# Halving the rounding of streamed weights, moving the root-table load, and single last results

## Chip, cores, metric

The kernel runs on one core of a Trainium2 chip. The metric is the device time of one execution in microseconds (us), the median of the runs shown. The profile is one further execution, taken by the hardware profiler. TensorE is PE in it (PEld its weight loads), VectorE is DVE, ScalarE is ACT, GpSimd is POOL, SyncE is SP.

## What is computed

Two networks in a row on 512 tokens of width 1024, all in float32. The first block is a feed-forward, then a mixer (RWKV-7 recurrence beside dilated attention), then a second feed-forward:

```python
x = x + 0.5 * swiglu(rms_norm(x, ffn1_norm), ffn1_w_in, ffn1_w_out)
h = rms_norm(x, mix_norm)
p_rwkv, p_q, p_k, p_v, p_gate = _split_last(h @ w_in, ...)
merged = g_a * (y_a @ w_proj_rwkv) + g_b * (y_b @ w_proj_attn)
x = x + merged @ w_out
x = x + 0.5 * swiglu(rms_norm(x, ffn2_norm), ffn2_w_in, ffn2_w_out)
```

The second block has two layers that also carry 256 context tokens (attention with low-rank and grouped keys, a convolution over 31 tokens, gates), and a last norm:

```python
for l in range(DEPTH_2):
    x, ctx = hybrid_layer(x, ctx, ...)
return rms_norm_2(x, final_norm_w)
```

`rms_norm` takes for each token the square root of the mean of squares. That root is what the word root table is about.

## The kernel before

Activations lie channels down, tokens across: `X` is 128 partitions x 8 tiles x 512 tokens, `XC` the context.

**Weights are streamed.** All weights of all stages are one stream of 336 blocks, each of 8 tiles (`UNITS`) of 128x128, 512 KB. Every block goes the same way through four engines, with two buffers for each step (slot = block number mod 2):

- SP fetches it into `RAW` (L2631) when POOL has finished the block two before (semaphore `split`).
- ScalarE copies it to `WHI`, rounded to the matmul's format (`round_block`, L312), when the fetch has landed and TensorE has used the block two before (`blocks_used`).
- POOL subtracts: `WLO` = `RAW` - `WHI`, the rest that rounding left (L2643 for the first two, L2647 in a loop), and raises `split`.
- TensorE waits for `split` in `block_ready` and forms the product in `product`: for each tile three matmuls, L324 (high weights, high activations), L325 (high, low) and L326 (low, high).

ScalarE's rounding isn't a program of its own. Each stage's scalar function calls `round_block` at fixed points of ScalarE's order, between the stage's own operations. So what ScalarE does ahead of a rounding delays the block, and a rounding delays what comes behind it. POOL does nothing else.

**Activations are split likewise.** In front of a feed-forward ScalarE writes `HHI` (L483) and VectorE `HLO` (L496), tile by tile; in front of the mixer and of a layer `HHI`/`HLO` and `H2HI`/`H2LO` come from a scaled copy (L421, L402/L404, L430/L432). The first product of each stage waits for them tile by tile.

**The order of the start.** SP issues: vectors, X tile 0, block 0, X tiles 1 and 2, the constants `SQC` (identity, ones, heads), X tiles 3 to 5, block 1, the others. ScalarE rounds block 0, then gains tiles 0 to 4, rounds block 1, gains tiles 5 to 7. TensorE's first instruction waits for `SQC`.

**Norms.** While the stage ahead ends, ScalarE squares each new tile of X (`squares`, L564) and VectorE adds the squares up (L579). Behind its last product TensorE sums over channels (`late_sums`, L352): first what VectorE has added, then the last tile's squares, for which it waits. VectorE adds both (L369, L371), ScalarE takes the root (L380), VectorE inverts it (L413), TensorE spreads it over the partitions (L375). The root needs another function table on ScalarE; a small root on a constant loads it first (L391 in `norm_scalar`, L2581 at the very end), right behind the last squares.

**The recurrence** (`rwkv_tensor` and its like) is a loop of four rounds, each for two pairs of heads. A round streams 18 blocks, mostly for modulation vectors (L874, L875), as filling between the small matmuls of the recurrence (L849). VectorE builds in it the matrices XIT and XI: a copy (L1247), a predicated copy with two inputs in SBUF (L1250), a transpose (L1255). At a round's end it normalises the outcome (L1203, L1211), and TensorE's next products wait for that.

**A layer** (`win_tensor`, `win_scalar`) begins with two blocks together, tile by tile as the norm delivers. From the third block on, TensorE waits for the copy and the squares (L2023, L2031) that ScalarE makes of the block two before, and ScalarE rounds ahead of those.

**The end.** VectorE makes eight result tiles (L2593), SP stores them in pairs (L2634).

## Time and profile before

| | |
|---|---|
| median of three runs | 2596.01 us (2595.64 to 2596.64) |
| the profiled execution's own time | 2598.18 us |
| its span | 2596.4 us |
| mean granted clock of TensorE | 0.986 |
| TensorE busy | 2475.2 us, 95% |
| VectorE busy | 1277.6 us, 49% |
| ScalarE busy | 1044.6 us, 40% |
| POOL busy | 809.4 us, 31% |

The busy shares are averages over stages that differ much. What counts is TensorE's idle time: the waits say how long it was and which instruction ended it. The granted clock is given as a share of full speed (2.4 GHz); 0.5 is the lower level (1.2 GHz). In the timeline a number in brackets is the time that the engine stood idle before the instruction, with what it waited for.

Where TensorE waits for the low parts of a weight block, and for XI, as the timeline shows it:

| place | TensorE starts again at | idle before it, us |
|---|---|---|
| first feed-forward, fifth block | 40.47 | 1.86 |
| low-rank prologue | 416.14 | 1.58 |
| low-rank prologue, four products later | 428.73 | 1.13 |
| layer 0, third block | 1744.66 | 3.56 |
| layer 1, third block | 2231.33 | 3.20 |
| XI, rounds 1 to 4 | 508.95, 642.94, 774.81, 909.41 | 2.26, 2.27, 2.26, 2.26 |
| end of rounds 1 to 3 (none in the fourth) | 580.28, 712.16, 846.76 | 2.90, 2.58, 3.22 |

The sixth wait for low parts is the second feed-forward's fifth block. Behind the four XI waits the granted clock was 0.51 (509.0 to 512.4), 1.00 (643 to 645), 0.54 (775 to 777) and 1.00 (911 to 913).

### The profile page before, as it was taken

How to read it: one execution, taken by the hardware profiler on the slowest of the kernel's cores; microseconds unless marked ns; L12 is line 12 of the kernel's file. 1: busy time of each engine (PE TensorE's matmuls, PEld its weight loads, DVE VectorE, ACT ScalarE, POOL GpSimd, SP SyncE). 2: the span in 40 equal slices, each digit the busy share in tenths (PEclk: the TensorE clock that was granted, in tenths of full speed). 3: DMA queues.
4: the chain of work that ended last, by engine and by line, in shares of the span. 5: the costliest groups of instructions: out<-in, count | busy, mean ns of one | idle time of the engine just before them, and what ended most of it. 6: DMA issues, size and time to landing. Idle time of an engine off the chain costs nothing.

```text
span 2596.4 us, 47970 instructions
## 1 busy us (share of the span) xinstructions
PE 2475.2 (95%) x18458; PEld 1984.9 (76%) x18458; DVE 1277.6 (49%) x2008; ACT 1044.6 (40%) x1836; POOL 809.4 (31%) x342
## 2 busy tenths in 40 slices
PE   7999999999999999999999999989999999898998
PEld 6888886877778787787878887878877668676776
DVE  3222224536363637555352222236777774577775
ACT  4222224434343434464342222233346552434762
POOL 3444443242424243223444444422221002233002
PEclk9999999999999999999999999989999999999999
DMA  4232333231313132112333323321110002122002
GB/s 138 94 97 89 105 98 96 63 93 56 97 59 92 57 100 73 57 50 80 103 120 97 96 89 97 105 65 49 57 52 30 1 2 64 42 73 73 18 2 73
DMA packets 52003, 188.43 MB, mean 73 GB/s; under 512 B 5760, under 2 KB 6016, under 8 KB 51712
## 3 DMA queue, kind: packets, MB, share of 16 engines
q1 hardware_dynamic: 50688, 181.74, 22.6%
q10 hardware_dynamic: 1152, 4.26, 0.5%
q8 instruction: 133, 2.18, 0.3%
q14 instruction: 30, 0.25, 0.0%
HBM read 183.88 MB, written 2.10 MB: 72 GB/s over the span
## 4 chain that ended last, share of the span: by engine, by line
issue 72%; POOL 15%; PE 9%; DVE 2%; ACT 1%; POOLq 1%; DVEq 0%; DMA 0%; SPq 0%; ACTq 0%
POOL WLO L2647 15%; PE psum L324 2%; PE psum L325 2%; PE psum L326 2%; PE psum L2385 1%; PE psum L2362 1%; PE psum L2400 1%; DVE psum L2190 1%; PE psum L2368 1%; DVE MX L2472 0%; DVE RN L2081 0%; POOLq L2644 0%; ACT PX L2438 0%; PE psum L2216 0%; DMA RAW<-in_wstream 0%
## 5 line engine op out<-in xcount | busy, mean ns | idle before, releaser
L2647 POOL TENSOR_TENSOR WLO<-RAW,WHI 128x1024 fp32r<-128x1024 f32 x334 | 804.4, 2409 | 1758.8 <-ACT WHI L312 1758.7
L312 ACT ACTIVATE WHI<-RAW 128x1024 fp32r<-128x1024 f32 x336 | 355.4, 1058 | 1027.8 <-PE psum L326 807.1
L324 PE MATMUL psum<-HHI,WHI 128*128 128x512 f32 x848 | 340.2, 401 | 18.5 <-DVE HLO L496 12.1
L325 PE MATMUL psum<-HLO,WHI 128*128 128x512 f32 x848 | 336.6, 397 | 0.0
L326 PE MATMUL psum<-HHI,WLO 128*128 128x512 f32 x848 | 336.4, 397 | 0.0
L324 PE MATMUL psum<-H2HI,WHI 128*128 128x512 f32 (+1 forms) x536 | 199.8, 373 | 14.2 <-DVE H2LO L430 7.4
L324 PEld LDWEIGHTS psum<-HHI,WHI 128*128 128x128 f32 x848 | 160.1, 189 | 59.9 <-issue 12.0
L325 PE MATMUL psum<-H2LO,WHI 128*128 128x512 f32 (+1 forms) x536 | 191.9, 358 | 0.0
L326 PE MATMUL psum<-H2HI,WLO 128*128 128x512 f32 (+1 forms) x536 | 191.4, 357 | 0.0
L325 PEld LDWEIGHTS psum<-HLO,WHI 128*128 128x128 f32 x848 | 160.3, 189 | 38.8 <-issue 1.2
L326 PEld LDWEIGHTS psum<-HHI,WLO 128*128 128x128 f32 x848 | 160.1, 189 | 38.7
L2438 ACT ACTIVATE PX<-psum,NM 128x512 f32<-128x512 f32 (+1 forms) x216 | 121.0, 565 | 93.9 <-DVE NM L2475 80.6
L324 PE MATMUL psum<-GHI,WHI 128*128 128x512 f32 x352 | 139.1, 395 | 0.9 <-DVE psum L641 0.9
L326 PE MATMUL psum<-GHI,WLO 128*128 128x512 f32 x352 | 139.0, 395 | 0.0
L325 PE MATMUL psum<-GLO,WHI 128*128 128x512 f32 x352 | 139.0, 395 | 0.0
L324 PEld LDWEIGHTS psum<-H2HI,WHI 128*128 128x128 f32 x536 | 102.9, 192 | 36.4 <-issue 11.6
L641 DVE TENSOR_TENSOR psum<-psum,FRSTD 128x512 f32<-128x512 f32 x44 | 30.8, 699 | 196.3 <-PE psum L326 196.0
L2472 DVE TENSOR_REDUCE MX<-psum 128x1 f32<-128x512 f32 (+1 forms) x216 | 107.9, 536 | 23.9 <-PE psum L2368 15.9
L325 PEld LDWEIGHTS psum<-H2LO,WHI 128*128 128x128 f32 x536 | 103.6, 193 | 18.0 <-issue 2.7
L326 PEld LDWEIGHTS psum<-H2HI,WLO 128*128 128x128 f32 x536 | 102.9, 192 | 15.9
L2385 PE MATMUL psum<-SQC,PX 128*128 128x128 f32 x624 | 89.1, 280 | 21.3 <-ACT PX L2438 13.7
L2385 PEld LDWEIGHTS psum<-SQC,PX 128*128 128x128 f32 x624 | 65.4, 140 | 43.4 <-issue 41.4
(418 smaller groups left out, 4914.3 us busy)
## 6 DMA issues: line engine op xcount, KB each, us to landing
RAW<-in_wstream SPq DMA_DIRECT2D x336, 512.0 KB, 3.5
X<-in_xT SPq DMA_DIRECT2D x8, 256.0 KB, 6.9
out_T<-OUT SPq DMA_DIRECT2D x4, 512.0 KB, 2.7
W3S<-in_lora ACTq DMA_DIRECT2D x5, 384.0 KB, 3.1
XC<-in_ctxT ACTq DMA_DIRECT2D x1, 1024.0 KB, 5.6
TRIG<-in_trig ACTq DMA_DIRECT2D x1, 960.0 KB, 7.5
FCC<-in_first SPq DMA_DIRECT2D x1, 576.0 KB, 8.7
LVL<-in_levels SPq DMA_DIRECT2D x1, 384.0 KB, 9.1
```

The source lines that it names most:

```text
L312: act.activation(WHI[:, q % 2, :], RAW[:, q % 2, :], ACT.Copy).then_inc(rounded, 1)
L324: pe.matmul(out, tile_of(WHI, slot, u), hi(kt), start=first and last[0], stop=False)
L325: pe.matmul(out, tile_of(WHI, slot, u), lo(kt), start=False, stop=False)
L326: mm = pe.matmul(out, tile_of(WLO, slot, u), hi(kt), start=False, stop=end and last[1])
L641: dve.tensor_tensor(up, up, FRSTD[:, :], ALU.mult).then_inc(*st.dve.inc(f"up{n}"))
L2190: dve.scalar_tensor_tensor(out=acc[i], in0=CIN[:, i, bass.ds(s + 1, span)], scalar=col(f"dw_w{l}", s + (i * CONV_K + 1)), in1=acc[i], op0= ...
L2362: pe.matmul(SCORES[a][:, at:at + w], QAM[:, i * 2 + a, qs], KAM[:, i * 2 + a, at:at + w], start=True, stop=True)\
L2368: mm = pe.matmul(SCORES[a][:, at:at + TC], QAG[hs, i, qs], KAG[hs, at:at + TC], start=True, stop=True)
L2385: mm = pe.transpose(TURNED[a][:, b * P:(b + 1) * P], PX[:, a, b * P:(b + 1) * P], eye)
L2438: act.activation(PX[:, a, c], SCORES[a][:, c], ACT.Exp, scale=scale_of(kind), bias=NM2[:, u % COLS:u % COLS + 1], accum_out=DEN2[:, cols]) ...
L2472: dve.tensor_reduce(MX2[:, cols], SCORES[a][:, c], AX, ALU.max).then_inc(*V.inc(f"mx{z}{u}"))
L2647: pool.tensor_tensor(WLO[:, s, :], RAW[:, s, :], WHI[:, s, :].bitcast(F32), ALU.subtract)\
```

## The change

- `round_block` writes `WHI` in two halves (4 tiles each), each raises `rounded`; POOL subtracts in halves, each raises `split`. All counts on `split` double.
- `block_ready` still asks for both halves. A new `half_ready` asks for the first, and `product` then waits for the second in front of its fifth tile. It is used for the second to fourth block of a feed-forward, in the low-rank prologue from its second block on, and from the third block of a layer on. The loops of the feed-forwards, the recurrence, attention and all the rest ask for whole blocks as before.
- The first fetch is two transfers. ScalarE gains tile 0 ahead of rounding block 0. `SQC` is fetched behind all tiles of X, and TensorE waits for it only before it first uses it.
- The small root (now `root_table`, on `EPS` into a tile `TABLE` of its own) stands ahead of the last tile's squares: in the feed-forwards' last step and in `out2_scalar`. For that the last step is taken out of ScalarE's loops. The one in the middle of a feed-forward (L597) stays.
- The last four result tiles are stored as one pair and two single tiles, five transfers in all.

```diff
+        HALVES = slice(0, UNITS // 2 * P), slice(UNITS // 2 * P, UNITS * P)
+
         def round_block(act, q, i=0, nb=0):
 
             act.wait_ge(raw_full[q % 2], 16 * (q // 2 + 1) + i * (8 * nb))
             if q >= 2:
                 act.wait_ge(k.blocks_used, q - 1 + i * nb)
-            act.activation(WHI[:, q % 2, :], RAW[:, q % 2, :], ACT.Copy).then_inc(rounded, 1)
+            for z, half in enumerate(HALVES):
+                if q == 0 and z == 1:
+                    act.wait_ge(second_in, 16)
+                act.activation(WHI[:, q % 2, half], RAW[:, q % 2, half], ACT.Copy).then_inc(rounded, 1)
...
-        def product(pe, out, slot, units, hi, lo, last, ready=None):
+        def product(pe, out, slot, units, hi, lo, last, ready=None, second=None):
...
+                if second and u == UNITS // 2:
+                    pe.wait_ge(*second)
...
         def block_ready(pe, q, i=0, nb=0):
-            pe.wait_ge(split, q + 1 + i * nb)
+            pe.wait_ge(split, 2 * (q + 1) + i * (2 * nb))
+
+        def half_ready(pe, q, i=0, nb=0):
+
+            pe.wait_ge(split, 2 * q + 1 + i * (2 * nb))
+            return split, 2 * (q + 1) + i * (2 * nb)
...
         def norm_scalar(act, nm, rounds={}):
             st = nm.st
-            act.activation(ROOTN[:, 2 * KB:], EPS[:, 0:2], ACT.Sqrt).then_inc(*st.act.inc("table"))
...
             for q in range(1, 4):
-                block_ready(pe, st.b0 + q)
+                second = half_ready(pe, st.b0 + q)
...
+                    if not f.updates:
+                        pe.wait_ge(const_in, 16)
...
+        def root_table(act):
+
+            if root_table.loaded:
+                act.wait_ge(tabled, root_table.loaded)
+            act.activation(TABLE[:, :], EPS[:, 0:2], ACT.Sqrt).then_inc(tabled, 1)
+            root_table.loaded += 1
...
+                        if n and isinstance(i, int) and i == FFN_OUT_LOOPS - 1:
+                            root_table(act)
                         squares(act, st, f.parts, n, i, f.squares[0])
             if f.updates:
-                with act.Fori(0, FFN_OUT_LOOPS) as i:
+                with act.Fori(0, FFN_OUT_LOOPS - 1) as i:
                     step(i)
+                step(FFN_OUT_LOOPS - 1)
...
             for c in range(1, PRO_BLOCKS):
-                block_ready(pe, st.b0 + c)
+                second = half_ready(pe, st.b0 + c)
...
                 if t >= 2:
-                    block_ready(pe, st.b0 + t)
+                    second = half_ready(pe, st.b0 + t)
...
         def out2_scalar(act, L):
             st = L.out
-            full = KT // 2 - (1 if L.last else 0)
+            full = KT // 2 - 1
...
-            if L.last:
-                round_block(act, st.b0 + KT)
-                for n in range(2):
-                    squares(act, st, L.sources, n, full, SQ_LATE[0])
+            for n in range(2):
+                if n == 0 or not L.last:
+                    round_block(act, st.b0 + n + KT)
+                if n:
+                    root_table(act)
+                squares(act, st, L.sources, n, full, SQ_LATE[0])
...
+        RESULTS = [(0, 2), (2, 4), (4, 6), (6, 7), (7, 8)]
...
-            sp.dma_start(RAW[:, 0, :], wstream[0]).then_inc(raw_full[0], 16)
+            for half, landed in zip(HALVES, (raw_full[0], second_in)):
+                sp.dma_start(RAW[:, 0, half], wstream[0][:, half]).then_inc(landed, 16)
             for t in range(1, KT):
                 sp.dma_start(X[:, t, :], xT[:, t, :]).then_inc(x_in[t], 16)
-                if t == 2:
-                    sp.dma_start(SQC[:, :], square).then_inc(const_in, 16)
                 if t == 5:
                     sp.dma_start(RAW[:, 1, :], wstream[1]).then_inc(raw_full[1], 16)
+            sp.dma_start(SQC[:, :], square).then_inc(const_in, 16)
...
-                    sp.wait_ge(split, i * 2 + (s - 1))
+                    sp.wait_ge(split, i * 4 + 2 * (s - 1))
                     sp.dma_start(RAW[:, s, :], wstream[i * 2 + s]).then_inc(raw_full[s], 16)
-            for z in range(4):
-                sp.wait_ge(*final.dve.at(f"out{2 * z + 1}"))
-                sp.dma_start(outT[:, 2 * z:2 * z + 2, :], OUT[:, 2 * z:2 * z + 2, :]).then_inc(out_done, 16)
-            sp.wait_ge(out_done, 4 * 16)
+            for t0, t1 in RESULTS:
+                sp.wait_ge(*final.dve.at(f"out{t1 - 1}"))
+                sp.dma_start(outT[:, t0:t1, :], OUT[:, t0:t1, :]).then_inc(out_done, 16)
+            sp.wait_ge(out_done, len(RESULTS) * 16)
...
-                    pool.tensor_tensor(WLO[:, s, :], RAW[:, s, :], WHI[:, s, :].bitcast(F32), ALU.subtract)\
-                        .then_inc(split, 1)
+                    for z, half in enumerate(HALVES):
+                        pool.wait_ge(rounded, i * 4 + (2 * s + z + 1))
+                        pool.tensor_tensor(WLO[:, s, half], RAW[:, s, half], WHI[:, s, half].bitcast(F32), ALU.subtract).then_inc(split, 1)
...
-            pe.wait_ge(const_in, 16)
             ffn_tensor(pe, ffn1)
...
+            gained_scalar(act, ffn1, 0)
             round_block(act, 0)
-            for t in range(KT):
+            for t in range(1, KT):
                 gained_scalar(act, ffn1, t)
```

The order of ScalarE's instructions at the start, before (the names: `WHI` is a weight block's high part, `HHI` an activation tile's):

```order
L312 ACTIVATE WHI<-RAW 128x1024 [waits raw_full0]
L483 ACTIVATE HHI<-X,VEC 128x512 [waits x_in0]
L483 ACTIVATE HHI<-X,VEC 128x512 [waits x_in1]
L483 ACTIVATE HHI<-X,VEC 128x512 [waits x_in2]
L483 ACTIVATE HHI<-X,VEC 128x512 [waits x_in3]
L483 ACTIVATE HHI<-X,VEC 128x512 [waits x_in4]
L312 ACTIVATE WHI<-RAW 128x1024 [waits raw_full1]
L483 ACTIVATE HHI<-X,VEC 128x512 [waits x_in5]
```

and of the change:

```order
L495 ACTIVATE HHI<-X,VEC 128x512 [waits x_in0]
L318 ACTIVATE WHI<-RAW 128x512 [waits raw_full0]
L318 ACTIVATE WHI<-RAW 128x512 [waits second_in]
L495 ACTIVATE HHI<-X,VEC 128x512 [waits x_in1]
L495 ACTIVATE HHI<-X,VEC 128x512 [waits x_in2]
L495 ACTIVATE HHI<-X,VEC 128x512 [waits x_in3]
L495 ACTIVATE HHI<-X,VEC 128x512 [waits x_in4]
L318 ACTIVATE WHI<-RAW 128x512 [waits raw_full1]
L318 ACTIVATE WHI<-RAW 128x512
L495 ACTIVATE HHI<-X,VEC 128x512 [waits x_in5]
```

Tile 0 of the activations went ahead of the first block, and each block is two instructions of 512 columns, of which only the first block's second has a wait of its own.

The same engine where the second feed-forward ends and layer 0 begins (`SQX`, `SQCTX` are the last tile's squares, `ROOTN` the norm's root; the first rows are the end of the loop's body), before:

```order
L561 REGISTER_ALU
L563 REGISTER_ALU [waits vector_steps]
L564 ISA [waits vector_steps]
L564 ACTIVATE SQX<-X 128x512
L563 REGISTER_ALU
L564 ISA [waits vector_steps]
L564 ACTIVATE SQCTX<-XC 128x256
L623 REGISTER_ALU
L623 COMPARE_AND_BRANCH
L391 ACT_TABLE_LOAD
L391 ACTIVATE ROOTN<-EPS 128x2 [waits ctx_in]
L380 ACTIVATE ROOTN<-ROOTN,EPS 128x12 [waits blocks_used,vector_steps,scalar_steps,tensor_steps]
```

and of the change:

```order
L318 ACTIVATE WHI<-RAW 128x512 [waits blocks_used,raw_full1]
L318 ACTIVATE WHI<-RAW 128x512
L318 ACTIVATE WHI<-RAW 128x512 [waits blocks_used,raw_full0]
L318 ACTIVATE WHI<-RAW 128x512
L584 ACT_TABLE_LOAD
L584 ACTIVATE TABLE<-EPS 128x2 [waits tabled]
L578 ACTIVATE SQX<-X 128x512 [waits vector_steps]
L578 ACTIVATE SQCTX<-XC 128x256 [waits vector_steps]
L393 ACTIVATE ROOTN<-ROOTN,EPS 128x12 [waits vector_steps,blocks_used,scalar_steps,tensor_steps,ctx_in]
```

The table load and the small root went from behind the last squares to ahead of them. In front of layer 1 it reads the same.

TensorE in the middle of a feed-forward's fourth block (fourth and fifth tile; `HHI`, `HLO` are the activations' parts), before:

```order
L324 MATMUL psum<-HHI,WHI 128x512
L325 MATMUL psum<-HLO,WHI 128x512
L326 MATMUL psum<-HHI,WLO 128x512
L324 MATMUL psum<-HHI,WHI 128x512
L325 MATMUL psum<-HLO,WHI 128x512
L326 MATMUL psum<-HHI,WLO 128x512
```

and of the change:

```order
L332 MATMUL psum<-HHI,WHI 128x512
L333 MATMUL psum<-HLO,WHI 128x512
L334 MATMUL psum<-HHI,WLO 128x512
L332 MATMUL psum<-HHI,WHI 128x512 [waits split]
L333 MATMUL psum<-HLO,WHI 128x512
L334 MATMUL psum<-HHI,WLO 128x512
```

The fifth tile's first matmul has a wait of its own, for the second half.

## Rows read from the trace of the kernel before

**Rows 1.** waits of TensorE: instruction <- releaser: us in total, times, longest

```profile
PE psum L324 <- POOL WLO L2647: 13.2, 6, 3.6
PE psum L849 <- DVE XI L1255: 9.1, 4, 2.3
```

**Rows 2.** page, part 5: busy us, mean ns | idle us before, releaser

```profile
L2647 POOL TENSOR_TENSOR WLO<-RAW,WHI 128x1024 fp32r<-128x1024 f32 x334 | 804.4, 2409 | 1758.8 <-ACT WHI L312 1758.7
```

**Rows 3.** timeline: start us, us, engine, line, operation [idle before <-releaser]

```profile
0.78 0.10 POOL L2640 MEMSET EPS<- 128x1 f32 x1
15.84 2.18 ACT L490 ACTIVATE SQ<-X 128x512 f32<-128x512 f32 x4
```

**Rows 4.** timeline, end of the first product

```profile
14.16 2.39 POOL L2643 TENSOR_TENSOR WLO<-RAW,WHI 128x1024 fp32r<-128x1024 f32 x1 [3.76 <-ACT WHI L312]
14.73 3.03 DVE L496 SCALAR_TENSOR_TENSOR HLO<-X,VEC,HHI 128x512 fp32r<-128x512 f32 x2 [1.14 <-ACT HHI L483]
17.16 0.50 PE L324 MATMUL psum<-HHI,WHI 128*128 128x512 f32 x1 [1.02 <-DVE HLO L496]
```

**Rows 5.** timeline of TensorE, behind the fourth block, then the prologue

```profile
40.47 0.50 PE L324 MATMUL psum<-HHI,WHI 128*128 128x512 f32 x1 [1.86 <-POOL WLO L2647]
...
416.14 0.50 PE L324 MATMUL psum<-HHI,WHI 128*128 128x512 f32 x1 [1.58 <-POOL WLO L2647]
```

**Rows 6.** windows: busy us of PE, PEld, DVE, ACT, POOL, granted clock

```profile
41.00:45.00 4.00, 4.00 (x12) 3.10 (x11) 0.56 (x1) 0.00 (x0) 1.75 (x1) 0.57 0.69 187
509.00:512.40 3.40, 3.40 (x40) 2.56 (x40) 0.88 (x2) 0.60 (x1) 0.00 (x0) 0.51 0.33 128
```

**Rows 7.** timeline, first round of the recurrence, around XI

```profile
503.89 1.06 ACT L312 ACTIVATE WHI<-RAW 128x1024 fp32r<-128x1024 f32 x1 [3.16 <-PE psum L875]
504.54 0.38 DVE L1247 COPY XIT<-FCC 128x512 f32<-128x512 f32 x1
505.03 2.35 POOL L2647 TENSOR_TENSOR WLO<-RAW,WHI 128x1024 fp32r<-128x1024 f32 x1 [7.89 <-ACT WHI L312]
505.08 2.88 DVE L1250 COPY_PREDICATED XIT<-LVL,MA 128x512 f32<-128x512 int32 x1 [0.15 <-DVE XIT L1247]
508.95 1.33 PE L849 MATMUL psum<-XI,MA 64*64 64x64 f32 x20 [2.26 <-DVE XI L1255]
```

**Rows 8.** timeline, VectorE between two POOL instructions in the prologue

```profile
414.80 1.84 DVE L835 TENSOR_TENSOR LDIF<-LP 128x512 f32<-128x512 f32 x1
416.04 2.86 POOL L2647 TENSOR_TENSOR WLO<-RAW,WHI 128x1024 fp32r<-128x1024 f32 x1
```

**Rows 9.** timeline, end of the first round of the recurrence

```profile
576.79 2.34 POOL L2647 TENSOR_TENSOR WLO<-RAW,WHI 128x1024 fp32r<-128x1024 f32 x1 [7.22 <-ACT WHI L312]
577.47 1.94 DVE L1211 TENSOR_SCALAR DV<-DV,VEC 128x512 f32<-128x512 f32 x1 [0.23 <-DVE DV L1203]
```

**Rows 10.** timeline, entry of the first layer, then the last root

```profile
1713.40 1.28 ACT L391 ACT_TABLE_LOAD   x1
1714.70 0.20 ACT L391 ACTIVATE ROOTN<-EPS 128x2 f32<-128x2 f32 x1
1713.53 0.71 PE L352 MATMUL psum<-SQC,SQX 128*128 128x2 f32 x4 [0.90 <-ACT SQCTX L564]
...
2585.22 0.30 ACT L380 ACTIVATE ROOTN<-ROOTN,EPS 128x8 f32<-128x8 f32 x1 [0.32 <-DVE ROOTN L371]
```

**Rows 11.** timeline, third block of layer 0 and of layer 1

```profile
1742.74 0.87 ACT L2031 ACTIVATE SQ<-psum 128x512 f32<-128x512 f32 x2
1744.66 0.76 PE L324 MATMUL psum<-H2HI,WHI 128*128 128x512 f32 x1 [3.56 <-POOL WLO L2647]
...
2229.15 0.59 ACT L2031 ACTIVATE SQ<-psum 128x512 f32<-128x512 f32 x1
2231.33 0.47 PE L324 MATMUL psum<-H2HI,WHI 128*128 128x512 f32 x1 [3.20 <-POOL WLO L2647]
```

**Rows 12.** page, part 6: DMA issues, KB each, median us to landing

```profile
out_T<-OUT SPq DMA_DIRECT2D x4, 512.0 KB, 2.7
```

More of the change, by code:

```diff
@@ L254, in block_kernel @@
         split = sem("split")
+        second_in, tabled = sem("second_in"), sem("tabled")
         x_in = [sem(f"x_in{i}") for i in range(KT)]
@@ L347, in __init__ @@
                     dve += [f"lo{g}_{t}"] + [f"h{g2}_{t2}" for g2, t2 in self.order[k_ + 2:k_ + 3]]
-                self.st = Stage(k, 0, ("sum", "spread"), ["table", "std"] + [f"hi{g}_{t}" for g, t in self.order], dve)
+                self.st = Stage(k, 0, ("sum", "spread"), ["std"] + [f"hi{g}_{t}" for g, t in self.order], dve)
         def token_sums(pe, blocks, out, src):
@@ L801, in lora_tensor @@
                     ready = lambda t: pe.wait_ge(*N.dve.at(f"lo0_{t}"))
-                product(pe, bank[c % 8], (st.b0 + c) % 2, ALLK, n_hi if raw else h_hi, n_lo if raw else h_lo, WHOLE, ready).then_inc(k.blocks_used, 1)
+                product(pe, bank[c % 8], (st.b0 + c) % 2, ALLK, n_hi if raw else h_hi, n_lo if raw else h_lo, WHOLE, ready, second).then_inc(k.blocks_used, 1)
         def lora_scalar(act, st):
@@ L1978, in win_tensor @@
                             pe.wait_ge(*L.norm.st.dve.at(f"lo1_{KT - 1}"))
-                        mm = product(pe, bank[b][:, 0:n], (st.b0 + t) % 2, ALLK, *tokens_of(at, n), WHOLE)
+                        mm = product(pe, bank[b][:, 0:n], (st.b0 + t) % 2, ALLK, *tokens_of(at, n), WHOLE, None, None if at else second)
                     mm.then_inc(k.blocks_used, 1)
@@ L2609, in block_kernel @@
             layers.append(Layer(l))
-        final = Stage(k, 0, ("sum", "spread"), ("table", "std"), ["first", "both", "rstd"] + [f"out{t}" for t in range(KT)])
+        final = Stage(k, 0, ("sum", "spread"), ("std",), ["first", "both", "rstd"] + [f"out{t}" for t in range(KT)])
         k.planned = k.blocks
```

12 lines of the change are left out of this document (6 added, 6 removed).

## Prediction, written before the changed kernel was run

> **What bounds the kernel now.** I read the engine shares first: TensorE is busy for 95% of the span, so a gain has to come out of its gaps, or out of stretches at the lower clock. Next the waits of TensorE, longest in total first. Two of its lines matter here [rows 1]: six waits for the low parts of a weight block (POOL, 13.2 us) and four for the transposed matrix XI of the recurrence (VectorE, 9.1 us). Then, for each, the instructions of the stretch in order of time.
>
> POOL needs 2.41 us a block [rows 2]. In the steady part of a feed-forward the next block is ready long before TensorE wants it, so halving there gives nothing; only the places of [rows 1] can pay. POOL also holds up VectorE. The predicated copy L1250 takes 2.88 us [rows 7] where it starts 0.05 us behind a POOL instruction; it ends 0.58 us behind that instruction's end (505.03 + 2.35 = 507.38). The Trainium skill, SBUF — State Buffer, "Who interferes with whom", has this as a rule: a VectorE operation with two SBUF inputs and a POOL operation that reads SBUF exclude each other for a whole instruction. The trace agrees, with those 2.88 us. So a POOL instruction of half the length also halves how long VectorE can be shut out.
>
> **The price of a half.** ScalarE: four operations of 128x512 take 2.18 us [rows 3], one 0.6 and each further one 0.5; a pair of halves takes 1.15 against 1.06 [rows 7], so 0.1 more. POOL: not less than half of 2.41, 1.2, and not more than 2.4. I take 1.25, near the lower end, since POOL's smallest instruction, a memset of one column, is 0.10 long [rows 3] and is the nearest row for a fixed part. From the start of rounding, a whole block was ready after 1.06 + 0.08 + 2.40 = 3.54 us; now the first half is ready after 0.6 + 0.1 + 1.25 = 1.95 and the whole after 3.2. So a wait for a whole block shrinks by 0.3, one for a first half by up to 1.6. The same skill, GPSIMD Engine Reference, section 3.1, measured 4497 ns for 2048 elements; with 2.35 for 1024 here that would put a half at about 1.3 (an estimate) and the sum 0.5 us higher.
>
> **The change, part by part.**
>
> *Start.* The last thing to hold up the first product is its sixth tile: TensorE waits until 17.16 for HLO [rows 4], whose operation began at 14.73, behind POOL's second block (14.16 to 16.55). The constants SQC no longer go ahead of block 1, which I take to land 0.4 us sooner; POOL's whole block ends 0.3 sooner. Both together: -0.8 for the sixth to eighth tile (bounds 0 and -1.7, all of the time from 15.5, when that operation would have ended unblocked). That TensorE may start a microsecond sooner is lost in waiting for that tile.
>
> *Feed-forwards.* Behind the fourth block TensorE waits 1.86 [rows 5], in the second feed-forward the same. The loop asks for a whole block, so -0.3 each: -0.6.
>
> *Low-rank prologue.* Waits of 1.58 [rows 5] and 1.13 (the table ahead). Here TensorE asks for a half, 1.6 sooner: the first wait goes (-1.5). The second hangs on ScalarE's sigmoids behind a VectorE chain, which doesn't move; TensorE reaches it 1.5 sooner, and the half takes 1.5 from it. Sum -1.5.
>
> *Recurrence, XI.* ScalarE starts to round at 503.89, POOL at 505.03, and L1250 wants the port at 505.08 [rows 7]. Now POOL would start at about 504.6 and the plain copy L1247, which I count among those that exclude POOL, at 504.54. If the copy is first, POOL's first half runs from 504.9 to 506.15 and L1250 is next, done at 506.9 instead of 507.96: -1.1. Does a waiting VectorE get the port between two POOL instructions? Yes by [rows 8]: the subtraction issued at 414.80 ends at 416.64, and the POOL instruction that starts at 416.04 lasts 2.86, some 0.45 over the usual, so VectorE went first. Four rounds with the same 2.3 us: -4.4 (bounds 0 and -5.8, four times 1.45, if POOL's half were free at 505.8).
>
> *Recurrence, end of a round.* L1211 is stretched to 1.94 by POOL from 576.79 to 579.13 [rows 9]. Behind it comes another operation with two SBUF inputs. One gets in between the halves, the other waits for the second half, whose end is 0.3 earlier: -0.3 in each of three rounds (the fourth has no wait), -1.0.
>
> *Root table.* ScalarE loads it right behind the last squares, at 1713.40 to 1714.9 [rows 10], and TensorE and VectorE sum meanwhile; at the very end ScalarE is ready 0.32 us before the root may start [rows 10]. So nowhere is the load on the path. Now it stands ahead of the last squares. In front of the two layers those squares start as soon as ScalarE has rounded, and TensorE waits for them (0.90 us, [rows 10]), so load, one small root and the dearer pair come in whole: 1.28 + 0.20 + 0.1 = +1.6, twice +3.2. In front of the mixer TensorE has other products meanwhile, and at the end ScalarE is idle before the last squares: 0 both times.
>
> *Third block of a layer.* TensorE waits until 1744.66 and 2231.33 [rows 11]. The half would be ready 1.6 sooner, but TensorE also needs the squares, done at 1743.61 and 2229.74, now 0.2 later. That leaves -0.8 and -1.3, sum -2.1. The cover that is next late is those squares.
>
> *Results.* The last transfer is 256 KB and not 512, of a landing of 2.7 us [rows 12]: -0.5 (bounds 0 and -1.3).
>
> *Clock.* After the gaps of 1.86 and of 2.26 the granted clock was 0.57 and 0.51 over 4.0 and 3.4 us [rows 6], that is the lower of the two levels (1.2 GHz), and cost some 1.7 us each. The table ahead shows it behind two of the four XI waits. Where a gap shrinks to about 1 us I expect some of these stretches to go; a gap of 1.58 had none. Three are at stake, 5.1 us. I take a third, -1.7.
>
> **Sum:** -0.8 - 0.6 - 1.5 - 4.4 - 1.0 + 3.2 - 2.1 - 0.5 - 1.7 = -9.4. The profiled execution took 2598.2 and would take 2588.8; the median of the runs shown is 2.2 lower, so 2586.6. A measurement of this kernel can tell about 0.2%, 5.2 us, from no change: faster is below 2590.8, slower above 2601.2.
>
> **The rivals.**
> - *POOL wins the port at XI.* The two starts, 504.54 and 504.6, are 0.06 us apart. If POOL is first, the copy goes between the halves, the second half takes the port at 506.1 to 507.35, and L1250 ends at about 508.05, as before. The XI term is 0 and its clock gains go: -9.4 + 4.4 + 1.1 = -3.9, 2592.1. For it: 0.06 us is little. Against: the copy is the earlier of the two.
> - *The clock comes back everywhere.* All three stretches vanish: another 3.4 us, 2583.2. For it: the gap of 1.58 was followed by full clock. Against: two of four equal gaps were, too, so that it isn't the gap's length alone.
> - *POOL's halves cost nearly a whole.* The place is POOL's queue, 668 instructions now. A whole block is ready later than before once a half takes more than (3.54 - 0.7) / 2 = 1.4 us. At 1.9 it is 1.0 later: the feed-forward waits grow by 2.0, the ends of the rounds by 3.0, the start by 1.0; XI gives nothing, prologue and layers give 0.9, 0.8 and 0.9, the results 0.5, and the table costs 3.2. Sum +6.1, 2602.1: slower. For it: no row has a POOL operation of this kind at 512 elements. Against: the 0.10 of the memset.
> - *The change does nothing for its parts' reasons.* The table load was hidden already, and most products still wait for whole blocks. Without any port effect only start, prologue, third block, results and table stand: -2.3, 2593.7, within the same.
>
> **How the numbers follow.** My forecast 0.42, POOL first 0.28, the full clock 0.15, dear halves 0.07, no port effect 0.08. The likeliest is 2586.6. The range reaches from the full clock with XI at its lower bound (2581.8), less a part of the start's bound, to just beyond POOL first and no port effect (2593.7): 2581 to 2595. It leaves out the dear halves and the tails. Faster by over 0.2%: most of the forecast (0.39), the full clock (0.15), a third of POOL first (0.1) = 0.64. Slower 0.06. Within: 0.30.
>
> **What would show it.** Right: POOL's instruction at 1.2 to 1.3 us, twice as many; the stretched L1250 at 1.8 instead of 2.88; TensorE's XI wait at 1.2; no wait for POOL in the prologue's first place; the table load between rounding and the last squares, with a TensorE wait for squares of 2.5 in both layers. Wrong: a half at over 1.4 us; XI waits still at 2.3; VectorE operations that are now shut out twice; or a root table that some engine was waiting for after all, seen as a wait before the root that is gone.

## The result and the profile after

| | before | after |
|---|---|---|
| median | 2595.82 us (2595.44 to 2596.64, 4 runs) | 2555.64 us (2550.39 to 2557.23, 4 runs) |
| the profiled execution's span | 2596.4 us | 2548.6 us |
| TensorE busy | 2475.2 us | 2434.8 us |
| ScalarE busy | 1044.6 us | 1074.7 us |
| VectorE busy | 1277.6 us | 1208.9 us |
| POOL busy | 809.4 us | 891.9 us |
| mean granted clock | 0.986 | 0.988 |

The changed kernel takes 0.9836 of the time before, 95% interval 0.9821 to 0.9852: 40 us less, where the prediction had 9 and at most 15. The forecast was wrong. Half of the answer stands in the row of TensorE's busy time: it does the same 18458 matmuls in 40.4 us less. (The profiled execution is the fastest of the four. That its span is 47.8 us shorter and not 40 is partly the clock: 65.1 us at the lower level in this trace, 75.6 in the one before, which at half speed is 5 us.)

The waits of TensorE after (us in total, times, longest):

```profile
PE psum L365 <- ACT SQCTX L578: 5.0, 2, 2.5
PE psum L332 <- ACT SQ L2056: 4.5, 2, 2.7
PE psum L332 <- POOL WLO L2676: 4.1, 3, 1.7
PE psum L874 <- DVE XI L1280: 3.8, 4, 0.9
```

The waits for low parts fell from 13.2 to 4.1 and those for XI from 9.1 to 3.8 [rows 1]. What stands above them now is forecast too: squares behind the table load, 2.5 us at each layer, and squares in front of a layer's third block. Up to here this is the forecast. Its parts on the page, POOL in the same columns as [rows 2]:

```profile
L2676 POOL TENSOR_TENSOR WLO<-RAW,WHI 128x512 fp32r<-128x512 f32 x668 | 886.1, 1348 | 1629.2 <-ACT WHI L318 1629.2
L332 PE MATMUL psum<-HHI,WHI 128*128 128x512 f32 x848 | 335.0, 395 | 14.1 <-POOL WLO L2671 8.7
L334 PE MATMUL psum<-HHI,WLO 128*128 128x512 f32 x848 | 331.1, 390 | 0.0
```

and the two TensorE groups before:

```profile
L324 PE MATMUL psum<-HHI,WHI 128*128 128x512 f32 x848 | 340.2, 401 | 18.5 <-DVE HLO L496 12.1 <-POOL WLO L2647 6.4
L326 PE MATMUL psum<-HHI,WLO 128*128 128x512 f32 x848 | 336.4, 397 | 0.0
```

A matmul record is 6 to 7 ns shorter. Does that show in the time? The steady part of the first feed-forward, 200 us in which TensorE is never idle, first before, then after (stretch, its length, TensorE busy and instructions begun, clock, DMA):

```profile
60.00:260.00 200.00, 200.00 (x859) 1.00 0.29 92
```

```profile
60.00:260.00 200.00, 200.00 (x884) 1.00 0.32 97
```

At full clock in both, 859 matmuls of 512 columns before, 884 after: 0.2328 and 0.2262 us each. In the timeline the step from one to the next is 0.233 before (119.80, 120.04, 120.27, 120.51) and 0.227 after (119.70, 119.93, 120.16, 120.38). Some 6,000 such matmuls follow one another without a gap; at 6.6 ns each that is up to 40 us, and nearly all of the large products have it. One tile was left out. The activations NHI of the mixer, after (records' least, middle and greatest ns, first and last start), and HHI beside them:

```profile
L332 PE MATMUL psum<-NHI,WHI x24: 392/392/482, 377.0 to 395.8; 128*128 128x512 f32 x24
L332 PE MATMUL psum<-HHI,WHI x848: 389/389/792, 8.7 to 1548.9; 128*128 128x512 f32 x170
```

NHI's row reads 392/392/482 before, too, and its steps are 0.234 in both traces. Its address didn't change either. The arena's did: the change adds a tile, `TABLE`, of 8 bytes a partition. It takes 32 bytes among the small fixed tiles, and the arena (the region behind them that holds HHI, GHI, H2HI and most other activations), rounded up to 64, begins at byte 69248 instead of 69184. The weights `WHI` and `WLO` lie ahead of `TABLE` and stay where they were; NHI is placed from the end of memory. That is theory A, the address. Its rival B: the shorter operations of POOL and ScalarE leave TensorE's reads in peace.

### The profile page after: what moved, and what is told of

Its sections match the earlier page's. It is cut to its first block and busy times, and to the rows that moved or that the text cites. A ratio compares the mean times of both kernels' runs of the same rounds, so it can differ in the third digit from the quotient of the medians.

```text
span 2548.6 us, 48956 instructions
## 1 busy us (share of the span) xinstructions
PE 2434.8 (96%) x18458; PEld 1982.8 (78%) x18458; DVE 1208.9 (47%) x2008; ACT 1074.7 (42%) x2172; POOL 891.9 (35%) x678
## 5 line engine op out<-in xcount | busy, mean ns | idle before, releaser
L2676 POOL TENSOR_TENSOR WLO<-RAW,WHI 128x512 fp32r<-128x512 f32 x668 | 886.1, 1348 | 1629.2 <-ACT WHI L318 1629.2
L318 ACT ACTIVATE WHI<-RAW 128x512 fp32r<-128x512 f32 x672 | 386.8, 623 | 972.1 <-PE psum L334 756.4
L332 PE MATMUL psum<-HHI,WHI 128*128 128x512 f32 x848 | 335.0, 395 | 14.1 <-POOL WLO L2671 8.7
L334 PE MATMUL psum<-HHI,WLO 128*128 128x512 f32 x848 | 331.1, 390 | 0.0
L333 PE MATMUL psum<-HLO,WHI 128*128 128x512 f32 x848 | 330.9, 390 | 0.0
L666 DVE TENSOR_TENSOR psum<-psum,FRSTD 128x512 f32<-128x512 f32 x44 | 30.8, 699 | 189.7 <-PE psum L334 189.6
L2410 PE MATMUL psum<-SQC,PX 128*128 128x128 f32 x624 | 89.0, 280 | 21.4 <-ACT PX L2463 14.4
```

The source lines that it names most:

```text
L318: act.activation(WHI[:, q % 2, half], RAW[:, q % 2, half], ACT.Copy).then_inc(rounded, 1)
L332: pe.matmul(out, tile_of(WHI, slot, u), hi(kt), start=first and last[0], stop=False)
L333: pe.matmul(out, tile_of(WHI, slot, u), lo(kt), start=False, stop=False)
L334: mm = pe.matmul(out, tile_of(WLO, slot, u), hi(kt), start=False, stop=end and last[1])
L666: dve.tensor_tensor(up, up, FRSTD[:, :], ALU.mult).then_inc(*st.dve.inc(f"up{n}"))
L2410: mm = pe.transpose(TURNED[a][:, b * P:(b + 1) * P], PX[:, a, b * P:(b + 1) * P], eye)
```

## The experiments

**1. The arena alone, 64 bytes up.** In the kernel before:

```diff
-        at[0] = -(-at[0] // 64) * 64
+        at[0] = -(-at[0] // 64) * 64 + 64
```

> The kernel before with one edit: everything behind the small fixed tiles (HHI, GHI, H2HI and all others of the arena) starts 64 bytes later, at 69248 and not 69184, as it does in the changed kernel, where the new tile TABLE pushed it there. Theory A (address): a 128x512 matmul whose moving tile lies at a multiple of 128 bytes follows the one before after 0.227 us, one that is 64 bytes off after 0.233; the trace of the changed kernel has 0.2267 everywhere but on NHI, whose address didn't move and which keeps 0.23 to 0.24. Then this kernel runs in 2553 to 2563 us, TensorE's busy time falls from 2475 to about 2437, and the waits of the kernel before (13.2 us on WLO, 9.1 on XI) stay. Theory B (halves): it is the shorter operations of ScalarE and POOL that leave TensorE's reads in peace. Then 2596 as before, cadence 0.233.

Measured: 2566.09 us (2564.78 to 2566.39), 0.9882 of before [0.9866, 0.9898]. TensorE busy 2441.8 us, 884 matmuls in 60 to 260 us, XI waits 9.1 and low-part waits 13.8 us. An edit that moves no work gave 30.8 us (against 2596.85, the kernel before measured beside it). B falls. It is 3 us outside my window. One reason is in experiment 4: matmuls of 256 columns got slower. Another is that a TensorE that arrives earlier waits longer: for CACC, which VectorE makes in each layer, 12.0 us and not 10.3.

**2. The whole change at the old addresses.**

```diff
-        EPS, TABLE = fixed("EPS", [P, 2]), fixed("TABLE", [P, 2])
+        EPS = fixed("EPS", [P, 2])
...
-            act.activation(TABLE[:, :], EPS[:, 0:2], ACT.Sqrt).then_inc(tabled, 1)
+            act.activation(ROOTN[:, 2 * KB:], EPS[:, 0:2], ACT.Sqrt).then_inc(tabled, 1)
```

> The changed kernel with its whole edit but without the new tile TABLE: the root table's load writes into ROOTN's spare columns as before, and the arena starts at 69184 again. Theory A (address): 2586 to 2592 us, that is before's 2596 less what halves, start, table and results give by themselves (forecast 2586.6), cadence 0.233. Theory B (halves): 2555 as the changed kernel, cadence 0.227.

Measured: 2586.59 us (2583.01 to 2587.51), 0.9961 [0.9947, 0.9975], 859 matmuls in the stretch. The two parts add up: 30.8 for the address and 10.3 for the edits, 41.1 together, against 40.2 for both at once (2595.82 - 2555.64). The XI waits are 3.8 us in total, as in the changed kernel: the halves do their work here, and the shorter step isn't part of it.

**3. 32 bytes up.** As experiment 1 with 32.

> The kernel before with the arena 32 bytes later, at 69216, 96 bytes off a multiple of 128 (where NHI lies in both traces, at 0.23 to 0.24 per matmul). Theory A in the form that only a multiple of 128 counts: 2596 as before. Theory A in the form that the distance to the weights or to other tiles counts, or that less offset is better: between 2560 and 2596. Theory B: 2596.

Measured: 2598.19 us, 1.0008 [0.9999, 1.0018]; 859 matmuls. No smooth effect of distance.

**4. The matmuls alone.** The kernel's work is left out. Eleven stages, each with a moving tile `M` and a stationary tile `W` at offsets of their own (in bytes, below as moving/stationary; at 0/0 the two lie 20 times 256 bytes apart), ran once:

```python
for M, W, n in views:
    for g in range(4):
        for j in range(24):
            mm = pe.matmul(bank[g][:, 0:n], W[:, j % 4, :], M[:, j % 2, 0:n], start=j == 0, stop=j == 23)
```

> The work of the kernel is left out altogether: 11 stages of 96 matmuls each in a row, with no other engine at work. Moving tile at 0, 64, 32, 96 bytes from a multiple of 128 with the stationary tile at 0 (MA to MD), then both moving and stationary at 0/64 and 64/64 (ME, MF), the four combinations again with 256 columns (MG to MJ), and the first again (MK). Theory A: 0.227 us from start to start in MA, ME and MK, 0.233 in MB, MC, MD and MF, with 256 columns 0.12 and about 0.127. If the stationary tile counts too, ME differs from MK. Theory B, or a cause in the other engines: all the same, 0.213 to 0.227.

Measured (TensorE's rows of the tiles):

```profile
L284 PE MATMUL psum<-MB,WB x96: 388/392/397, 51.5 to 73.3; 128*128 128x512 f32 x96
L284 PE MATMUL psum<-MC,WC x96: 389/394/397, 73.5 to 95.7; 128*128 128x512 f32 x96
L284 PE MATMUL psum<-ME,WE x96: 394/394/394, 118.3 to 140.5; 128*128 128x512 f32 x96
L284 PE MATMUL psum<-MF,WF x96: 388/389/398, 140.7 to 162.3; 128*128 128x512 f32 x96
L284 PE MATMUL psum<-MG,WG x96: 279/283/283, 162.5 to 173.9; 128*128 128x256 f32 x96
L284 PE MATMUL psum<-MH,WH x96: 278/279/282, 174.0 to 185.2; 128*128 128x256 f32 x96
L284 PE MATMUL psum<-MI,WI x96: 276/276/282, 185.3 to 196.1; 128*128 128x256 f32 x96
L284 PE MATMUL psum<-MK,WK x96: 388/389/397, 207.7 to 229.3; 128*128 128x512 f32 x96
```

Last start less first, by 95 steps, all at full clock: MK (0/0) 0.227, MF (64/64) 0.227, MB (64/0) 0.229, MC (32/0) 0.233, ME (0/64) 0.233. Nothing else runs, so no other engine is involved, and the stationary tile counts as much as the moving one: my form of A, the moving tile alone, was wrong. With 256 columns the order turns round: 0.120 at equal offsets (MG), 0.118 with the moving tile 64 above (MH) and 0.114 with it 64 below (MI). So what gains 6 ns a piece at 512 columns loses 2 to 6 at 256.

**5. The grid.** The same with 20 stages of 48, of 512 columns, once: moving and stationary tile at 0, 32, 64 and 96 in all combinations, then 128 or 256 apart.

> The kernel's work is left out: 20 stages of 48 matmuls of 512 columns each, no other engine at work. MV is a warm-up. MA to MD: moving tile at 0, 32, 64, 96 bytes from a multiple of 128 with the stationary tile at 0; ME to MH the same with the stationary tile at 32; MI to ML at 64; MM to MP at 96; MQ, MR, MS: one of the two, or the moving one, moved by 128 or 256 instead. Theory A2 (the two addresses relative to each other, from the run before: 0/0 and 64/64 227 ns, 32/0, 96/0 and 0/64 233, 64/0 229): the diagonal MA, MF, MK, MP 227 ns, all others 229 to 233, and MQ, MR, MS 227. Theory A1 (each operand for itself has to lie at a multiple of 64): MA, MK 227, MF and MP 233.

Measured, from each stage's first start to the next one's, by 48:

```profile
L282 PE MATMUL psum<-MA,WA x48: 389/389/389, 41.1 to 51.8; 128*128 128x512 f32 x48
L282 PE MATMUL psum<-MB,WB x48: 393/396/399, 52.0 to 63.0; 128*128 128x512 f32 x48
L282 PE MATMUL psum<-MF,WF x48: 389/389/395, 96.6 to 107.3; 128*128 128x512 f32 x48
L282 PE MATMUL psum<-MG,WG x48: 393/396/399, 107.5 to 118.5; 128*128 128x512 f32 x48
L282 PE MATMUL psum<-MP,WP x48: 389/389/397, 207.9 to 218.5; 128*128 128x512 f32 x48
L282 PE MATMUL psum<-MQ,WQ x48: 390/394/398, 218.8 to 229.7; 128*128 128x512 f32 x48
L282 PE MATMUL psum<-MR,WR x48: 390/394/398, 230.0 to 240.9; 128*128 128x512 f32 x48
L282 PE MATMUL psum<-MS,WS x48: 387/389/398, 241.2 to 251.9; 128*128 128x512 f32 x48
```

0.227 on the diagonal, where both offsets are equal (MA, MF, MP; MK alike), and 0.233 or 0.234 beside it (MB, MG), but for the two places where the moving tile is 64 above the stationary one (MC, MH, 0.229). MQ and MR, 128 bytes apart, are slow, MS, 256 apart, is fast: so my expectation of 227 for MQ and MR fell. The fast pairs of this grid are those whose addresses differ by a multiple of 256 bytes. In the kernel WHI lies at 41088 and WLO at 49280, both 128 above a multiple of 256; HHI lay at 69184, 64 above one, and now lies at 69248, 128 above. So the distance went from 64 short of a multiple of 256 to a multiple of 256.

**6. The weights 64 bytes up.** In the kernel before, `CS` (64 bytes) stands in front of `X`; the arena stays.

> The kernel before with the small tile CS put in front of X, so that X, RAW, WHI, WLO and SQC lie 64 bytes later and the arena stays where it was: now weights and moving tiles are both 64 bytes off a multiple of 128. Theory A2 (relative): the cadence of 128x512 falls to 0.227 and the time to about 2566, as with the arena moved, but NHI's 72 matmuls stay at 0.233. Theory A1 (moving tile alone): 2596 as before.

Measured: 2596.31 us, 0.9999 [0.9989, 1.0008]; 859 matmuls. Expected was 2566, from the first four experiments, which didn't tell 128 from 256. Weights and HHI are now 128 apart, as in MQ: slow, in agreement with the grid. It alone doesn't exclude that the arena's own address counts.

**7. The weights 192 bytes up.** `MX2` and `NM2` (192 bytes) in front of `X`.

> The kernel before with MX2 and NM2 (192 bytes) in front of X: the arena stays, the weights lie 192 bytes later. The grid run and the run with the weights 64 bytes later say that the fast cadence comes where the two addresses differ by a multiple of 256; here HHI is at 69184 and WHI at 41280, 27904 = 109 x 256 apart, before 28096. Theory A3 (difference a multiple of 256): cadence 0.227 in the arena's products, 2562 to 2568, without a byte of the arena moved. Rival (the arena's own address, multiples of 128 or 256 of it, counts in the whole kernel): 2596.

Measured: 2566.43 us (2565.83 to 2566.93), 0.9881 [0.9866, 0.9896]; 884 matmuls, TensorE busy 2439.5 us. The same as in experiment 1, with not a byte of the arena moved. What counts is the difference of the two addresses. Why it does, no run here says.

**8. The root table back.** In the changed kernel `root_table(act)` is called at the start of `norm_scalar` and `final_scalar`, and no more in the last steps.

> The changed kernel with one part undone: the root table is loaded behind the last squares again, at all four places (TABLE stays, and with it the addresses). By my terms the two layers lose their +1.6 and +1.4, and the third blocks, which the squares now hold up, gain what those came too late by: 2555.6 - 3.2 = 2552.4, TensorE's waits for SQCTX 2 x 0.9 and not 2 x 2.5. Rival: with the load behind the squares it is on the path to the root, as before it wasn't: 2555.6 or more.

Measured: 2549.22 us (2546.73 to 2552.43, 5 runs), 0.9817 [0.9804, 0.9830], against 2555.64. At the entry of layer 0, changed, then with the table back:

```profile
1671.82 1.28 ACT L584 ACT_TABLE_LOAD   x1
1673.12 0.20 ACT L584 ACTIVATE TABLE<-EPS 128x2 f32<-128x2 f32 x1
1674.29 1.84 PE L365 MATMUL psum<-SQC,SQX 128*128 128x2 f32 x8 [2.50 <-ACT SQCTX L578]
```

```profile
1672.27 1.28 ACT L585 ACT_TABLE_LOAD   x1
1672.39 1.84 PE L365 MATMUL psum<-SQC,SQX 128*128 128x2 f32 x8 [0.98 <-ACT SQCTX L579]
```

TensorE's wait for the last squares is 1.5 us shorter at each layer, 3.0 in all, where 3.2 was forecast. The medians differ by 6.4. All five executions of this version lie between 2546.73 and 2552.43, while those of the change and of experiments 9 and 10, which keep the table's new place, lie between 2550.39 and 2557.23, so the difference is there, but its second half isn't explained. It isn't the clock at the layers' entries: from there the lower level lasted 13.65 us in layer 0 and 10.24 in layer 1 in both traces. Of all parts that were undone here, the table's new place is the one that costs.

**9. Whole waits.** In the changed kernel `half_ready` waits for both halves.

> The changed kernel with one part undone: TensorE waits for both halves of a block everywhere, the start of each product included, while ScalarE and POOL still work in halves. By my terms it loses the prologue's first wait (1.6 of which comes back) and up to 0.9 and 1.3 in front of the third blocks, +2 to +4 us: 2558 to 2559; the XI waits stay at 0.9, since they come from the port and not from the half wait. Rival (first halves do the whole work): XI waits go back to 2.3 each, 2564 or more.

Measured: 2555.75 us (2553.03 to 2556.92), no difference from 2555.64. In the traces the prologue's first wait is back by 0.66 us, the second by 0.40, and the third blocks come 0.57 and 1.12 later; these 2.8 us lie within the spread of the executions. XI waits stay at 3.8 in total. By the traces the first-half waits are worth some 3 us; the medians don't show it.

**10. The start undone.** Block 0 in one transfer, `SQC` ahead, the order of before.

> The changed kernel with its start undone: block 0 fetched whole, the constants ahead of block 1, ScalarE rounding ahead of its first tile, TensorE waiting for the constants; halves, table and results as changed. In the trace of the change at the old addresses the end of the first product came 1.6 us earlier than in the kernel before; of this the halves of POOL and ScalarE should give 0.3 or more, so 0.5 to 1.4 are lost: 2556 to 2557, and the first matmul again at about 11 us instead of 9. Rival: the eighth tile ends the first product in both, no difference at 25 us.

Measured: 2554.60 us (2552.79 to 2556.57), 0.9836 [0.9821, 0.9851]: no difference. TensorE starts at 10.61 and not 8.66, and its second product at 18.43 against 18.78 changed (19.37 before). The rival has the time right but not the reason. Starting at 8.66, TensorE waits for the sixth and the seventh tile (0.58 and 0.73 us); starting at 10.61 it runs through the first product without a wait. Either way it arrives at the second at the same time within 0.4 us, and the new start brings nothing that shows.

**11. POOL whole.** In the changed kernel POOL waits for both halves of WHI, subtracts a whole block and raises `split` by 2.

> The changed kernel with POOL's subtraction of whole blocks again (ScalarE still rounds in halves; WLO is ready as a whole only). My mechanism at XI is POOL's length against the predicated copy: POOL at 2.4 us instead of twice 1.27, the copy stretched to 2.9 again, the four XI waits 2.3 instead of 0.9 (+5.2), the stretches at the lower clock behind them back (+3), the prologue's wait back (+1.5), third blocks +2: about 2566. Rival: the gain at XI comes from ScalarE or from a shift in time, and XI waits stay at 0.9: 2560 or less.

Measured: 2562.69 us (2560.93 to 2564.26), 0.9868 [0.9852, 0.9883]. That is 7 us more than the changed kernel. The prologue (2.3) and the third blocks (1.0 and 1.6) came back, the fifth blocks (0.4 each) and the waits for CACC (0.5 and 1.4) too, but XI did the reverse of what I had said: only 0.1 of a wait is left in each round where the changed kernel has 0.94. In the first round:

```profile
493.40 0.73 DVE L1275 COPY_PREDICATED XIT<-LVL,MA 128x512 f32<-128x512 int32 x1 [0.15 <-DVE XIT L1272]
493.51 2.81 POOL L2674 TENSOR_TENSOR WLO<-RAW,WHI 128x1024 fp32r<-128x1024 f32 x1 [7.89 <-ACT WHI L318]
```

ScalarE's two halves take 0.09 longer than one whole, so POOL now comes behind the predicated copy, and the copy, 0.73 instead of 2.88 [rows 7], isn't held up. So POOL's halves are worth 7 us in all, although they cost 3.3 at XI (the places named make 4.3 of the 7; the rest wasn't followed up). New question: does half a length pay at XI, or coming second (P)?

**12. One tenth of a microsecond.** The kernel before, POOL untouched; only in front of a round's first XI does ScalarE round in two instructions:

```diff
-            act.activation(WHI[:, q % 2, :], RAW[:, q % 2, :], ACT.Copy).then_inc(rounded, 1)
+            at = UNITS // 2 * P if in_two else 0
+            if in_two:
+                act.activation(WHI[:, q % 2, 0:at], RAW[:, q % 2, 0:at], ACT.Copy)
+            act.activation(WHI[:, q % 2, at:], RAW[:, q % 2, at:], ACT.Copy).then_inc(rounded, 1)
...
-                    round_block(act, st.b0 + b + 2, i, LOOP_BLOCKS)
+                    round_block(act, st.b0 + b + 2, i, LOOP_BLOCKS, b == M_AT[0])
```

> The kernel before; only in front of the first XI of a round does ScalarE round its block in two instructions, with one release at the end of the second, so that POOL, as long as ever (2.35 us), starts 0.1 us later, behind the predicated copy instead of 0.05 us ahead of it. Theory P (who is first at the port): all four XI waits fall from 2.26 to about 0.1, the copy from 2.88 to 0.73, and two or three stretches at the lower clock go: 2596 - 8.6 - 3 = 2585. Theory H (the half length of a POOL instruction is what pays): no change, 2596.

Measured: 2583.23 us (2581.28 to 2584.84), 0.9949 [0.9934, 0.9964]. Of each XI wait 0.1 us is left.

```profile
504.47 0.74 DVE L1253 COPY_PREDICATED XIT<-LVL,MA 128x512 f32<-128x512 int32 x1 [0.15 <-DVE XIT L1250]
504.51 2.89 POOL L2650 TENSOR_TENSOR WLO<-RAW,WHI 128x1024 fp32r<-128x1024 f32 x1 [7.98 <-ACT WHI L315]
```

POOL comes 0.04 behind the copy where it had come 0.05 ahead, and 13.8 us are won (2597.04 - 2583.23), more than by all edits of the change together. The four waits account for 8.6 of them and shorter waits at the ends of rounds for 0.9; the rest is mostly clock, 65.1 us at the lower level in this trace against 75.6 in the one before.

**13. The best version.** The changed kernel with the table back and NHI at a multiple of 256 from the weights, first alone:

> The changed kernel with the root table loaded behind the last squares again, and with NHI and NLO 96 bytes lower, where they too are a multiple of 256 away from the weights. By theory A3 their 72 matmuls gain 6 ns each, 0.4 us; the table's part gives 3.0 by the two traces: 2552, and by the medians so far 2549. It should beat both kernels.

Measured: 2550.08 us (2542.86 to 2551.52), 0.9811 [0.9797, 0.9824], as experiment 8 within its spread. NHI's records are now as short as HHI's (392 ns above), and its steps are 0.227:

```profile
L332 PE MATMUL psum<-NHI,WHI x24: 389/389/486, 376.1 to 394.4; 128*128 128x512 f32 x24
```

Then with POOL released in front of a round's first XI for both halves together:

```diff
-                act.activation(WHI[:, q % 2, half], RAW[:, q % 2, half], ACT.Copy).then_inc(rounded, 1)
+                half_done = act.activation(WHI[:, q % 2, half], RAW[:, q % 2, half], ACT.Copy)
+                if not together:
+                    half_done.then_inc(rounded, 1)
+            if together:
+                half_done.then_inc(rounded, 2)
```

> The version with the root table back and NHI moved, in which POOL is released at that same place for both halves together, at the end of ScalarE's second. Theory P: POOL comes behind the predicated copy, the four XI waits fall from 0.94 to 0.1, -3.4 us against that version's 2550.1: 2546.7. Theory H: 2550 or a little more, since the first half is released later.

Measured: 2544.86 us (2542.86 to 2546.07, 5 runs), 0.9800 [0.9786, 0.9813]: faster than both kernels, 11 us below the change and 5 below the version without this edit, of which the XI waits are 3.3.

```profile
488.09 0.73 DVE L1278 COPY_PREDICATED XIT<-LVL,MA 128x512 f32<-128x512 int32 x1 [0.15 <-DVE XIT L1275]
488.14 3.02 POOL L2678 TENSOR_TENSOR WLO<-RAW,WHI 128x512 fp32r<-128x512 f32 x2 [8.26 <-ACT WHI L318]
```

## Why the prediction was right and wrong

**The step that failed** is no term of the sum but one that is missing from it. "In the steady part of a feed-forward the next block is ready long before TensorE wants it, so halving there gives nothing": true of halving, but I took it that nothing else changes there, and that TensorE could only gain "out of its gaps, or out of stretches at the lower clock". The matmul's own step was counted as fixed. It depends on where its operands lie, and the diff moves them: `EPS, TABLE = fixed("EPS", [P, 2]), fixed("TABLE", [P, 2])` is a new tile ahead of the arena, in a layout that is counted out. I named `TABLE` as a tile "of its own" and asked only when it is written. What the runs showed in its place: the step falls from 0.233 to 0.227 us, which is worth 30.8 us in experiment 1 and 31.1 in experiment 7, three quarters of the 40. The size of this effect couldn't be had from the trace before, in which all large products lie at slow distances (NHI too). A hint could: the step was 0.233, and 512 columns at one a cycle of 2.4 GHz are 0.213, an estimate that experiment 4 bears out (256 columns more cost 0.227 - 0.120 = 0.107). None of my cases had room for the effect: the lowest, the full clock everywhere with XI at its bound, ended at 2581.8.

**The steps of the sum**, read where the addresses are as before (experiment 2: median 10.3 us below before, forecast 9.4; the two profiled executions, 2598.18 and 2583.79, are 14.4 apart, so the column on the right, with smaller steps left out, holds about 4 us more than the medians give). Each number is by how much TensorE gets ahead of the kernel before at that place (minus), or falls back (plus):

| step | forecast | measured |
|---|---|---|
| start, to the second product | -0.8 | -1.6 (19.37 to 17.82) |
| fifth blocks | -0.3, -0.3 | -0.3, -0.3 |
| low clock behind the first of them | (clock) | -1.5: granted 0.69 before over 40.5 to 46, here 1.00 |
| prologue's two waits | -1.5 | -1.8, -0.8, then +1.7 by the lower clock, 0.72 over 442 to 448 |
| XI | 4 x -1.1 | 4 x -1.3 |
| low clock behind XI | (clock) | -1.5 each in rounds 1 and 3: all four at 1.00 here |
| ends of rounds | 3 x -0.3 | -0.4, -0.9, -1.6; the waits themselves 8.7 before, 7.7 here, the rest is mostly clock |
| attention, one stretch at the lower clock more | none | +1.5 |
| root table | +1.6, +1.6 | +1.9, +1.8 (the waits for squares +1.6, +1.4), and +1.2, +0.4 by the clock behind them |
| third blocks | -0.8, -1.3 | -0.9, -1.4 |
| a wait for CACC in each layer | none | -0.3, -1.5, and -1.0 by the clock behind the first; in total the wait is 10.3 before, 12.0 in experiment 1, 8.4 here |
| a wait for VAG, of VectorE too, in layer 1 | none | +0.9 |
| results | -0.5 | +0.1: from the last result tile to the end 3.04 before, 3.12 here |
| POOL's half | 1.25 us | 1.29 as a rule, 1.35 in the mean, which counts those that wait for the port |
| ScalarE's pair | 1.15 us | 1.15 |

That the forecast of the edits alone comes within 1 us of 10.3 is in part luck. The terms for XI, fifth blocks, ends of rounds and third blocks hold, but the wait for CACC (1.9 us less) wasn't in the sum, the wait for VAG wasn't either, and the terms for clock and results, 2.2 us together, came to nothing.

- *Start*: in experiment 2 twice my term, but experiment 10 says that the new order of the start isn't its reason. What is left is the halves and when X lands, which I haven't taken apart, and the start differs from run to run (second product at 18.71 in experiment 1, 19.37 before, with the same start). The term is not settled better than to 1 us.
- *Prologue*: I had it that the second wait stays. It shrank by 0.8, and a stretch at the lower clock behind it took the gain back.
- *XI*: right in size, wrong in mechanism by half. "If the copy is first, POOL's first half runs from 504.9": POOL does not wait for the end of the plain copy. Changed, copy L1272 runs from 490.30 to 490.69, and POOL's first half begins at 490.37 and ends at 491.82 nonetheless; the predicated copy ends at 492.41, so at 0.73 us alone it had the port from 491.68, 1.31 behind POOL's start, which is about the usual length of a half. It goes in between the halves, as I had said, and POOL's pair takes 3.13 instead of about 2.5. The copy takes 1.57 us, where I had 1.8, and the wait left is 0.94, where I had 1.2. But halving was only the lesser remedy. Experiments 11 to 13 show that all but 0.1 of the 2.3 us go if POOL comes second, and what decides is 0.1 us. The 0.05 us between the two starts stood in [rows 7]; I used it as doubt about my own term (the rival "POOL wins the port at XI", 0.28) and didn't see in it the cheaper change.
- The Trainium skill, SBUF — State Buffer, section "Who interferes with whom", says of the pair of ports that VectorE and GpSimd share that the order of issue decides who blocks. The traces agree: the predicated copy takes 2.88 us with POOL ahead and 0.74 with POOL behind, and then it is POOL that takes longer, 2.89 instead of 2.35.
- *Clock*: I had -1.7 of 5.1. The three stretches that I named did go, 4.5 us, but others came: in the prologue, in attention, and at the entry of layer 0. The lower level lasted 75.6 us in all before and 75.5 in experiment 2: the term is nothing. The entry of layer 0, before and in experiment 2 (TensorE busy, clock):

```profile
1711.00:1731.00 20.00, 15.29 (x76) 0.74 0.18 53
```

```profile
1698.00:1718.00 20.00, 13.70 (x56) 0.57 0.16 50
```

- *Root table*: right place and size of the load. That the clock behind it cost 1.6 us more in experiment 2 can't be put down to it. At the entry of layer 0 the lower level lasted 13.65 us in a row in the changed kernel, and just as long with the table back (experiments 8 and 13); with the table in its new place but POOL whole (experiment 11) it lasted 6.83, as before the change. What decides there is open.
- *Results*: a term without a ground. The last transfer is half as long in bytes, but from issue to landing 256 KB took 2.69 to 2.74 us and 512 KB 2.62 to 2.69, so nothing is gained.
- *Third block*: right, and the squares are now what is late, as forecast.
- *POOL's half*: the prediction's second estimate, 1.3, was nearer than the 1.25 that it used.
- *A list that doesn't fit its sum*: the rival without any port effect names start, prologue, third block, results and table, which make -1.7. Its -2.3 holds only with the feed-forwards' -0.6.
- The rivals: dear halves (2602.1) and no port effect (2593.7) are refuted by experiment 2 and its trace, POOL first by the XI waits of 0.9. The full clock everywhere, at 0.15, came true behind XI and the fifth block, but not as a gain in time.

## What to carry to other kernels

When a change allocates or drops a tile in a layout counted out, list the addresses that move before reading anything else, and compare the step of back-to-back matmuls with columns over clock: what is above it is worth a question, though not all of it can be had (0.227 against 0.213 was the best of all runs here). Try the operands' distance by padding alone, once, for the column count that bears most of the time. Where two engines share a port and start within 0.1 us of each other, try coming second before making either one shorter.

## What was not expected of the hardware

- Matmuls of 128x512 in this number format follow each other after 0.227 us where moving and stationary tile are a multiple of 256 bytes apart, after 0.229 where the moving one is 64 above that, and after 0.233 or 0.234 at all other distances tried (multiples of 32, up to 128). It is so with all other engines idle; the kernel shows 0.227 at a multiple of 256 and 0.233 at 64 and 32 below one and at 128.
- With 256 columns it is the other way round: 0.120 at equal offsets, 0.118 and 0.114 with the moving tile 64 above and 64 below. In the kernel the context's 600 matmuls of that width went from 0.117 to 0.120. But the distance isn't all there: at the same 64 below, the 256-column steps of `YHI` are 0.118 in the kernel before and 0.114 in experiment 2. Why wasn't found out; other distances at 256 columns weren't tried alone, nor other formats.
- A 64-byte shift was worth three times the edits it came with. How much more a layout gives that serves 512 and 256 columns each with its own distance wasn't tried either.
